# A 2-layer mixer trunk on 8 cores: norm of the first stage applied at PSUM, other order of first loads, first 24 weight blocks stored one pass later

## The reference

```python
def rmsnorm(x, g):
    y = xf * lax.rsqrt(jnp.mean(xf * xf, axis=-1, keepdims=True) + EPS)
    return y * g
...
for layer in range(2):
    xn = rmsnorm(h, mix_norm_g[layer])
    if layer == 0:
        p = xn @ ab_w_in                      # (B,T,2048)
        a, xb, gate_b, gate_c = split(p, 512) # four times 512 columns
        a_out = pool_mixer(a, pool_w, pool_scale)       # trailing means over 2/4/8/16 positions
        b_out = gate_b * short_conv(gate_c * xb, conv_w, conv_b)
        mix = concat([a_out, b_out]) @ ab_w_out
    else:
        ...   # gated MLP mixer and stick-breaking attention, then cd_w_out
    h = h + mix
    hn = rmsnorm(h, mlp_norm_g[layer])
    h = h + square(relu(hn @ mlp_w1[layer])) @ mlp_w2[layer]
return rmsnorm(h, final_norm_g)
```

## Time and profile before

| | |
|---|---|
| time, median of 3 runs | 2921.53 us (2921.23 to 2926.58) |
| the profiled execution | 2921.85 us |
| its span on the slowest core (core 5) | 2920.1 us |
| PE busy | 2797.7 us, 96% of the span |
| DVE, ACT, POOL busy | 49%, 43%, 55% |
| 16 DMA engines, mean rate | 144 GB/s |
| weight loads with cast (L622, POOL) | 180 of 256 KB |
| stores of blocks as bf16 (SP) | 180 |
| loads of bf16 blocks (SP) | 540 |

### The profile page before, as it was taken

The page is one execution under the profiler, slowest core; times in us unless marked ns, Lnnn a source line. Parts: engine busy times, 40 slices in busy tenths (PEclk is TensorE's granted clock), DMA queues, the critical chain, the costliest instruction groups (busy, mean ns, idle before and its releaser), DMA issues.

```text
span 2920.1 us, 43942 instructions; the slowest of 8 cores (2896.3 to 2920.1 us)
## 1 busy us (share of the span) xinstructions
PE 2797.7 (96%) x13211; PEld 1194.9 (41%) x13211; DVE 1436.4 (49%) x1759; ACT 1261.6 (43%) x2062; POOL 1602.0 (55%) x1793
## 2 busy tenths in 40 slices
PE   8999999999999999799998999999999989999998
PEld 3444444444443344343443444444444434444443
DVE  4411246464435555776645454445565675554003
ACT  3433234736335344365543353433645464444231
POOL 4655515765417777576761465550576766674333
PEclk9999999999999999899999999999999999999999
DMA  8798883456665999746755344465355485446222
GB/s 171 157 208 196 177 216 90 120 150 147 184 155 107 193 177 175 190 123 157 167 139 155 85 107 113 114 157 170 92 123 123 106 216 135 114 114 184 86 77 83
DMA packets 491478, 420.24 MB, mean 144 GB/s; under 512 B 310128, under 2 KB 334960, under 8 KB 491248
## 3 DMA queue, kind: packets, MB, share of 16 engines
q1 hardware_dynamic: 465184, 370.07, 49.1%
q0 software_dynamic: 26064, 47.36, 11.3%
HBM read 304.23 MB, written 89.13 MB: 135 GB/s over the span
## 4 chain that ended last, share of the span: by engine, by line
PE 79%; DMA 6%; DVE 6%; issue 4%; POOL 3%; ACT 2%; SPq 1%; DVEq 0%; POOLq 0%; ACTq 0%
PE ps L588 74%; PE ps L1349 3%; PE ps L1402 2%; DMA stg<-xT 2%; DMA ring<-wblk 1%; DVE vt L1209 1%; DVE P L1365 1%; DMA h<-xT 1%; POOL Wq L1379 1%; DMA Wk<-Wq 1%; SPq L581 1%; DVE X L746 1%; POOL ps L1064 1%; DMA ring<-wbf 1%; POOL ffB L937 0%
## 5 line engine op out<-in xcount | busy, mean ns | idle before, releaser
L588 PE MATMUL ps<-X,ring 128*128 128x512 bf16 x6144 | 1399.1, 383 | 36.3 <-DVE X L746 11.1
L588 PEld LDWEIGHTS ps<-X,ring 128*128 128x128 bf16 x6144 | 586.0, 98 | 778.9 <-issue 121.5
L1379 POOL TENSOR_TENSOR Wq<-P 128x1024 bf16<-128x1024 f32 (+2 forms) x320 | 529.1, 1655 | 299.3 <-DVE P L1365 289.7
L588 PE MATMUL ps<-mix,ring 128*128 128x512 bf16 x2816 | 657.0, 380 | 7.2 <-POOL P L1360 4.1
L1365 DVE TENSOR_TENSOR_SCAN P<-ps,carry,cbs 128x512 f32<-128x512 f32 x384 | 488.9, 1279 | 346.1 <-POOL P L1360 200.6
L578 ACT ACTIVATE ps<-ps 128x512 f32<-128x512 f32 (+3 forms) x576 | 429.6, 750 | 477.4 <-PE ps L588 238.2
L588 PE MATMUL ps<-ffB,ring 128*128 128x512 bf16 x2048 | 485.1, 380 | 0.0
L811 DVE TENSOR_TENSOR tmp<-ps,ms 128x512 f32<-128x512 f32 x256 | 175.3, 685 | 494.0 <-PE ps L588 493.3
L816 POOL TENSOR_TENSOR h<-tmp,h 128x512 f32<-128x512 f32 x224 | 287.7, 1284 | 229.9 <-DVE tmp L811 229.1
L588 PEld LDWEIGHTS ps<-mix,ring 128*128 128x128 bf16 x2816 | 263.8, 98 | 339.7 <-issue 39.6
L1365 DVE TENSOR_TENSOR_SCAN P<-ps,cbs 128x128 f32<-128x128 f32 (+3 forms) x256 | 208.1, 819 | 323.6 <-ACT ps L578 189.4
(11 more groups left out here) (82 smaller groups left out, 1755.2 us busy)
## 6 DMA issues: line engine op xcount, KB each, us to landing
ring<-wbf SPq DMA_DIRECT2D x540, 256.0 KB, 3.0
ring<-wblk POOLq DMA_DIRECT2D x180, 256.0 KB, 7.9
wbf<-ring SPq DMA_DIRECT2D x180, 256.0 KB, 6.4
stg<-xT SPq DMA_DIRECT2D x96, 256.0 KB, 4.8
h<-xT SPq DMA_DIRECT2D x64, 256.0 KB, 7.4
hsp<-h SPq DMA_DIRECT2D x64, 256.0 KB, 3.7
h<-hsp SPq DMA_DIRECT2D x64, 256.0 KB, 6.2
oT<-mixf SPq DMA_DIRECT2D x32, 256.0 KB, 5.1
```

Of the source, the lines that this page charges most:

```text
L588: ins = pe.matmul(out, lhsT=l, rhs=r, start=(first and i == 0), stop=(last and i == n - 1), skip_group_check=True)
L1379: yield Req("pool", lambda e: e.tensor_tensor(out=W4, in0=P[:, :, 1:w + 1].rearrange("p h (j n) -> p h j n", n=128), in1=P[:, :, 0:w].rear ...
```

## The change

1. In the first stage, x is not normed ahead of the projection. `start_chunk` writes x times the norm's weight as bf16 (DVE), squares each chunk (ACT) into a free buffer and adds pairs (DVE); `start_norm` makes r squared and r. The projections run on the unnormed tile; r squared is applied where xb leaves PSUM and r where the pooled part does (both on DVE, ACT before), and r once more to the convolution's result, on POOL, ahead of the product with gate_b.
2. The first four weight loads wait for chunks 1 and 4 of half 0 and chunks 5 and 7 of half 1. Blocks of the first step are taken one by one. x for the next unit and the constants of layer 1 are gated on results of the first stage.
3. The first 24 blocks are not stored in the first pass. In the second (stage F01) they are loaded with cast by POOL again, and stored then.
4. Planned durations and DMA costs get other values, for the whole program.

```diff
-DMA_KB_US = 256.0
+DMA_KB_US = 230.0
...
-            if n < 8:
-                gate = [self.Lh[3][0]] if n < 4 else [self.Lh[3][1]]
+            if n < 4:
+                gate = [(self.Lh[1][0], self.Lh[4][0], self.Lh[5][1], self.Lh[7][1])[n]]
                 yield lambda: gate[0].w is not None
...
-            if b not in self.Lwbf:
+            if b not in self.Lwbf and n >= 24:
                 self.Lwbf[b] = LT("wbf")
                 self.busy.add(slot)
                 self.M.spawn(self.keep_block(slot, b), 0.5)
...
+    def start_chunk(self, t, c, sums):
...
+        yield Req("dve", lambda e: e.tensor_scalar(out=X[:, c, ts], in0=h, scalar1=g, scalar2=None, op0=ALU.mult),
+                  L + [self.Lcf], [LX[c][t]], 0.55)
+        self.xl[t] += 1
+        yield lambda: t == 0 or i in sums[0]
+        yield self.act(self.Vf[:, c, :], h, AF.Square, L, [self.LV[2 * c], self.LV[2 * c + 1]], TT, False)
+        if odd:
+            yield Req("dve", lambda e: e.tensor_tensor(out=self.qT[:, i, ts], in0=self.Vf[:, c - 1, :], in1=self.Vf[:, c, :],
+                                                       op=ALU.add),
...
+    def start_norm(self, t, sums):
...
+        yield Req("act", lambda e: e.activation(out=m2, in_=m, func=AF.Exp, scale=-1.0), [self.Lms[ms]], [self.Lms[ms2]], 0.65)
+        yield Req("act", lambda e: e.activation(out=m, in_=m, func=AF.Exp, scale=-0.5), [], [self.Lms[ms]], 0.65)
...
+    def scaled(self, out, bk, ms, L):
+        return Req("dve", lambda e: e.tensor_tensor(out=out, in0=self.bank(bk), in1=self.ms[:, ms, :], op=ALU.mult),
+                   [self.Lms[ms]], [self.Lbank[bk], L], 0.70)
...
+            if late:
+                ms = self.rl[t][0]
+                yield Req("pool", lambda e: e.tensor_tensor(out=Y[:], in0=Y[:], in1=self.ms[:, ms, :], op=ALU.mult),
+                          [self.Lms[ms]], [LY], 1.29)
...
-        yield Req("pe", zmm, [self.LqT[a][tq], self.LkT[a][c]], Lz, w / 2400.0 + 0.07, bias=-0.04, wslack=0.5)
+        yield Req("pe", zmm, [self.LqT[a][tq], self.LkT[a][c]], Lz, w / 2400.0 + 0.37, bias=-0.04, wslack=0.5)
...
-                  [LWq], [LWk[r]], 1.25, key=("wk", k, r), lat=4.0, kb=w * 0.69)
+                  [LWq], [LWk[r]], 1.22, key=("wk", k, r), lat=1.6, kb=w * 0.4)
```

More of the change, by code:

```diff
@@ L689, in square @@
             yield Req("pool", lambda e: e.tensor_tensor(out=Xf[:, SQ[i][odd], hs], in0=sq, in1=sq, op=ALU.mult), Ls,
-                          [LX[k][t] for k in rows[odd]], 1.15, bias=0.5)
+                          [LX[k][t] for k in rows[odd]], 1.06, bias=0.5)
         else:
@@ L814, in evac @@
             self.banks.free(bk)
-            eng, d = ("dve", 0.70) if last and c >= 6 else ("pool", 1.15)
+            eng, d = ("dve", 0.71) if last and c >= 6 else ("pool", 1.29)
             yield Req(eng, lambda e: e.tensor_tensor(out=self.h[:, c, ts], in0=self.tmp[:, b, :], in1=self.h[:, c, ts],
@@ L871, in start_x @@
             yield r
+        self.xready.update(((0, 0, 0), (0, 0, 1)))
+        self.xl = [0, 0]
+        sums = [set(), set()]
         for t in range(2):
-            ts = slice(t * TT, (t + 1) * TT)
             self.hcount[("F", 0, 0, t)] = 8
[L875 to L882, removed]
@@ L883, in start_x @@
-            yield from self.norm(0, t, 0, self.to_X(t, 0), ev, [(c, c + 1) for c in range(4)])
-            self.xready.add((0, 0, t))
+            for c in range(8):
+                self.M.spawn(self.start_chunk(t, c, sums), -0.5)
+            self.M.spawn(self.start_norm(t, sums[t]), -0.5)
+    def start_chunk(self, t, c, sums):
+        X, LX = self.X[0], self.LX[0]
+        ts = slice(t * TT, (t + 1) * TT)
+        i, odd = divmod(c, 2)
+        h, L = self.h[:, c, ts], [self.Lh[c][t]]
+        g = self.cf[:, c:c + 1]
+        yield Req("dve", lambda e: e.tensor_scalar(out=X[:, c, ts], in0=h, scalar1=g, scalar2=None, op0=ALU.mult),
[6 more added lines that the diff above has]
+                                                       op=ALU.add),
+                      self.LV[2 * c - 2:2 * c + 2], [self.LqT[i][t]], 0.72)
+            sums[t].add(i)
@@ new lines, in start_norm @@
+    def start_norm(self, t, sums):
+        ts = slice(t * TT, (t + 1) * TT)
+        ms = yield self.p_ms
+        ms2 = yield self.p_ms
+        m, m2 = self.ms[:, ms, :], self.ms[:, ms2, :]
+        bk = yield (self.banks,)
+        for i in range(4):
+            yield lambda: i in sums
+            yield self.mm(self.bank(bk), [(self.cb[:, 0:128], self.qT[:, i, ts])], [self.LqT[i][t], self.Lones],
+                          [self.Lbank[bk]], i == 0, i == 3, bias=-0.05)
+        yield Req("act", lambda e: e.activation(out=m, in_=self.bank(bk), func=AF.Ln, scale=1.0 / D, bias=self.cf[:, 60:61]),
+                  [self.Lcf], [self.Lms[ms], self.Lbank[bk]], 0.72)
+        self.banks.free(bk)
+        yield Req("act", lambda e: e.activation(out=m2, in_=m, func=AF.Exp, scale=-1.0), [self.Lms[ms]], [self.Lms[ms2]], 0.65)
+        yield Req("act", lambda e: e.activation(out=m, in_=m, func=AF.Exp, scale=-0.5), [], [self.Lms[ms]], 0.65)
+        self.rl[t] = (ms, ms2)
+        yield lambda: self.mixn[t] == 8
+        self.p_ms.free(ms)
+        self.p_ms.free(ms2)
@@ L1050, in evac @@
         def evac(bk):
-            yield self.act(A[:, 16:528], self.bank(bk), AF.Copy, [], [self.Lbank[bk], LA], TT, True)
+            if late:
+                yield lambda: t in self.rl
+                yield self.scaled(A[:, 16:528], bk, self.rl[t][0], LA)
+            else:
+                yield self.act(A[:, 16:528], self.bank(bk), AF.Copy, [], [self.Lbank[bk], LA], TT, True)
             self.banks.free(bk)
@@ L1099, in stage_F @@
         for i in range(4):
-            sl = yield from self.take(4)
+            sl = [] if n == 0 else (yield from self.take(4))
             g = 3 - i
```

39 lines of the change are left out of this document (25 added, 14 removed).

## The result

The changed kernel took 2942.43 us in the median (2939.87 to 2949.64) beside 2921.38 for the kernel before: ratio 1.0075, 95% interval 1.0054 to 1.0095. It is some 22 us slower. The prediction, 2913.5 and faster, was wrong in size and in sign.

The account below looks back on a forecast made before the run. PE, busy 96% of the slowest core's span, was taken as the bound, so only its idle or lower-clock time could be won. -13.1 + 3.8 + 1.0 = -8.3 from 2921.85 gave 2913.5 us, range 2901 to 2927.

Parts of the forecast that it names:

- A: First step of the first stage: half 1 lands earlier and projection need not wait for the norm factor; -13.1 us (-15.4 to -4.4).
- the lower bound: Cheaper weight loads at the start, 1.76 us each instead of 3.2, so half 1 lands at 28.9 us, not 25.2.
- Rival 1: At the start, half 1's landing moves little and DVE's backlog adds 5 us: 2922.3 us, no change; chance 0.19.
- B: The other seven step halves: PSUM banks held while DVE waits for POOL's product; +3.8 us, from 0 to 20.
- Rival 3: POOL's product becomes the first stage's bound, 8 times 2.5 us: 2929.8 us, slower; chance 0.10.
- E: Other planned durations, whole program: attention's matmuls move by one or two groups; 0 us, +-8.
- C: First pass, 24 stores fewer: no slot is short; 0 us, from -1.0 to +1.0.
- D: Second pass, 24 cast loads more, issued by POOL; +1.0 us, from 0 to 30.
- the cover: POOL's 36.5 us free in 440 to 520 us fits ten extra issues and their waits for PE, 25.8 us.
- Rival 2: At the start, loads are held up by DVE's scaling, 3.9 us later: 2917.4 us, no change; chance 0.06.
- The rule of the Trainium skill: POOL cannot write its DMAs' descriptors while DVE runs in two-port mode; loads at the start up to 3.9 us later.

Follow-up runs that it names:

- old_post: The changed kernel with old planned numbers and DVE's gate_b product straight from PSUM, POOL's r product behind it; mean span -6.3 us against before, ratio 1.0003.
- old_consts: The changed kernel with all planned durations, bandwidth and latency numbers put back to those of before; mean span -2.3 us against before, ratio 0.9985.

## Why the prediction was wrong

**A, the start: right.** Forecast -13.1, measured -11.4 (53.7 to 42.3). In the changed kernel the last chunk of x is issued at about 18.5 us and takes 7.2 us to land (first row), and the timeline of ACT has the last four squares of half 1 (second row):
```profile
h<-xT SPq DMA_DIRECT2D x1, 256.0 KB, 7.2
```
```profile
25.71 2.17 ACT L579 ACTIVATE Vf<-h 128x512 f32<-128x512 f32 x4
```
Half 1 had thus landed by about 25.7 (forecast 25.2, by the lower bound 28.9), the projection went on at 29.73 (29.1), and the 64th matmul was done at 42.5 (41.8). Only the fourth block was dearer than thought: issued at 26.25 it took 7.5 us and landed at 33.8 (forecast 30.6), for 0.55 us of wait. Rival 1 (2922.3) is out.

**B, the other steps: place right, size wrong.** The price was put at four times 0.95, 3.8 us, from eight waits over the whole program, none of which lies between 50 and 160 us. With the old numbers 10.2 were given back, with the new ones 14.7. The bank held behind POOL's product was the larger part, 6.4, as old_post shows. What the step left out: DVE's own sums ahead of the product take twice as long beside POOL's adds, the kind of collision that the earlier trace rows showed of L793, and in the longest wait it was they, not the adds in POOL's queue, that held the product up; the lower clock behind such a wait, which the sum has for A and not for B; and the copies that I moved to DVE at no cost bring waits of 1.8. Rival 3 had the right place; at 10.2 in seven halves, 1.5 each, its 2.5 was too dear. That its 2929.8 lies nearer to the measured time is no merit of its mechanism, since most of the loss is E's.

**C and D, the stores and loads: right to within a few us, with the sign turned.** Forecast +1.0 together; with the old numbers the second pass is the better place by 4.4, in one pair of plans. POOL's busy time in 440 to 520 us, as sum of four windows of the changed kernel, against the earlier trace rows:
```profile
sum 80.00, PE 78.53 PEld 34.03 DVE 51.20 ACT 35.07 POOL 53.76; mean PE 19.63 PEld 8.51 DVE 12.80 ACT 8.77 POOL 13.44
```
POOL is busier by 10.2 (forecast some 14) and PE by 1.0, and no wait of PE there is longer than 0.8 us: the cover held.

**E, other planned durations: the step that failed.** "They move attention's matmuls by one or two groups" was right, two groups for AV. "0; a single wait like the 8.2 us behind L1077 may come or go, so +-8" was not: the new numbers cost 18.8 us alone, and 21 to 26 on the changed kernel (18.7 to 24 beside -2.3). The error was to look at the norms, which indeed kept their waits (L701 29.8, L702 30.5 now), and to take the rest as noise around nothing. The kernel before had 5.5 us of idle ahead of attention's first matmuls and 0.6 ahead of AV, in 400 groups: there was next to nothing for a new order to win, and much to lose. It also went unasked whether the new numbers fit the trace; those of attention's matmuls do not. Through which waits each group of numbers costs what it does stays open. With E at nothing the sum gives 2913.5; old_consts, which is the change without E, stands at -2.3 us of mean span where the forecast was -8.3. B's extra 6.4 is of that size, but C and D went 5.4 the other way, so some 5 us of this are not accounted for.

**Rival 2, loads held up by DVE's scaling: not seen.** The timeline of POOL in the changed kernel has its issues at a steady price while DVE scales (L888, rows from 25.41 to 28.6):
```profile
24.99 0.53 POOL L623 DMA_DIRECT2D ring<-wblk  x1 [12.58 <-DMA h<-xT]
26.25 0.53 POOL L623 DMA_DIRECT2D ring<-wblk  x1 [0.73 <-DMA h<-xT]
...
27.29 1.60 POOL L623 DMA_DIRECT2D ring<-wblk  x3
```
0.53 an issue, where the earlier trace rows have 0.58. The landing is not later either. The load issued at 26.25, the first of six like the one at 30.85 before, takes 7.5 us, where that one, with no such scaling beside it, takes 7.8:
```profile
ring<-wblk POOLq DMA_DIRECT2D x1, 256.0 KB, 7.5
```
The rule of the Trainium skill that was weighed there ("SBUF — State Buffer", "SBUF: two separate sides") showed no price in this stage.

## What to carry to other kernels

Where a planner sets the order, the numbers it plans with are a change of the whole program: their cost cannot be read from the stage that is being worked on, and it should be forecast with a range of its own (here -1 to +19 us for eight sets on the same kernel), or be kept out of the change and tried by itself. A planned number nearer to the trace is no better by that: the transposes' shorter time and POOL's measured sum both cost 8 us or more. But one that moves away from the trace, as those of attention's matmuls did, is best seen before the run: read the pace from starts, not from durations that overlap. And where a factor is moved behind a matmul, apply it after the instruction that frees the PSUM bank, not ahead of it.

## What the runs showed of the hardware

DVE's sum of two float32 tiles (L1062, L1065) takes 1.57 us beside POOL's adds and 0.75 us without them: two engines that the plan has side by side at full speed slow each other down. In old_consts (core 7) the 42 such sums with no long POOL operation on tiles beside them take 0.73 to 0.80 us, the 20 that run beside one for 0.3 us or more 1.4 in the median and 1.65 at most. DVE's operations that read PSUM do not slow: 215 products and sums out of a bank (L789, L812) with such a POOL operation beside them stay at 0.69 us or less.

And a transpose's landing has a long tail: 2.8 us in the median, 21.7 at most on core 1 of the kernel before. SP can also be slow to issue one. On core 4 of the changed kernel an issue takes 1.2 us in the median (first row: shortest, median and longest in ns, of 320). The two issued from 1020.08 on, around the start of PE's 13.6 us wait, take 12.0 us (second row). The second of them lands 8.3 us after its issue began (third row), at 1037.3, just ahead of the matmuls that waited (fourth row). Why SP was slow there is not shown.
```profile
L1442 SPq DMA_TRANSPOSE Wk<-Wq x320: 1167/1232/8782, 447.2 to 2641.7; - x160
```
```profile
1020.08 12.01 SPq L1442 DMA_TRANSPOSE Wk<-Wq  x2
```
```profile
Wk<-Wq SPq DMA_TRANSPOSE x1, 8.3
```
```profile
1037.43 1.92 PE L1456 MATMUL ps<-Wk,V 128*64 128x512 bf16 x8 [13.57 <-DMA Wk<-Wq]
```
